# The sub-norm weights of differential attention, applied in the copies out of the turned blocks

## The chip, the cores and the metric

One core of one Trainium2 chip runs the whole program. The metric is device time in microseconds (us) of one execution; the number quoted for a kernel is the median of several runs.

## The reference, cut to what matters

The program runs six layers over 256 tokens of width 1024, all in fp32: two hybrid layers (the second with a mixture of eight experts), then a layer of differential attention, one of block attention, one of sliding-window attention, and differential attention again. The change touches the two differential layers (numbers 2 and 5 of the kernel). What they compute after the attention itself is this:

```python
def rms_norm(x, g):
    xf = x.astype(jnp.float32)
    y = xf * lax.rsqrt(jnp.mean(xf * xf, axis=-1, keepdims=True) + NORM_EPS)
    return (y * g.astype(jnp.float32)).astype(x.dtype)

def diff_attention(...):
    ...
        p = p[:, :, 0] - lam * p[:, :, 1]
        return jnp.einsum('bhqk,bkhe->bqhe', p.astype(v.dtype), v)
    ...
    o = rms_norm(o, sub_g) * (1.0 - lambda_init)
    return o.reshape(B, S, H * DIFF_V_DIM) @ w_out
```

There are 8 heads of 128 columns. The weights `sub_g` are 128 numbers, the same for all heads, one for each column of a head.

## The kernel before, in words

**Products.** Every product with a weight matrix is made of three fp32r products. A unit of weights (128x2048) is loaded by the queue of SP into one of six buffers `raw`; ScalarE rounds it into `whi` (`hi`, line 1691, or half a unit at a time at line 1695), VectorE takes the remainder into `wlo` (`lo`, lines 2116 and 2122), and TensorE adds high by high, low by high and high by low. The activations are split in the same way: rows of `y` are turned by TensorE into a bank of PSUM, ScalarE copies the bank, rounded, into `xt_hi`, VectorE subtracts that from the bank into `xt_lo`. For the output product of attention these three steps are the three functions named `turn_mixed` (lines 798, 1711 and 2140), called for s = 0 to 3. In a differential layer s = 0 and 1 turn heads 0 to 3 of the first and of the second half of the tokens, s = 2 turns heads 4 and 5 and s = 3 heads 6 and 7, for all tokens. After turning, a partition of `xt` holds one column of a head.

**Attention in a differential layer** (`soft_heads`, 16 score maps in 8 pairs) is software-pipelined by hand: each engine has its own written-out order of steps. TensorE computes scores (lines 1593 and 1595), VectorE masks them and takes maxima (line 2551), ScalarE takes exponentials with row sums (lines 1821 and 1823), VectorE takes reciprocals (line 2500), GpSimd makes the ratio of the two maps (`ratio`, lines 711 and 712), VectorE combines the pair in two instructions (`combine`, line 2471), TensorE turns the combined map (`turn_pair`, line 1568), ScalarE copies it (line 1839), TensorE multiplies by the values (`pair_values`, lines 1580 to 1582), and VectorE scales the result into `y` (`finish_pair`, line 2482), sums its squares (line 2486) and asks GpSimd for a root (line 2150). In between TensorE does the last parts of the projection of the layer (line 843).

**The sub-norm** is `diff_norms` on GpSimd. For each head it makes the ratio of a later head, the root (line 692), then two passes over the head's 128x256 block of `y`: a multiplication by the root of each row (line 729) and one by the weights (line 730). The second raises `normed`, on which TensorE's `turn_mixed` waits (after 4, 4, 6 and 8 heads). The weights come in `subg`, 2 x 128 numbers copied to all partitions by one transfer (line 594, in `small`), and are scaled once by 1 - lambda_init (line 2425).

**Output product.** `out_project_diff` (line 977) orders the work of TensorE after the last pair: rows of the first half of the tokens for units 0 and 1, `turn_mixed` for s = 2, a part for the second half, `turn_mixed` for s = 3, then unit 2 once the low part of s = 2 is there and unit 3 once that of s = 3 is there. ScalarE and VectorE come to the two halves of unit 3 (`hi` and `lo` with halves) only after their own part of `turn_mixed` for s = 3.

```python
            for h in range(8):
                if h + 2 < 8:
                    ratio(l, h + 2)
                r = done[0]
                roots(1)
                pool.wait_ge(root_ready, r + 1)
```

Of the kernel before, what the change touches and what calls it, by code (L numbers as in the profile page):

```python
# [6 lines left out]
F32 = mybir.dt.float32  # L7
# [7 lines left out]
P = 128  # L15
# [157 lines left out]
def build(nc, A, out, bias_scratch):  # L173
    with ExitStack() as ctx:  # L174
        def sb(name, shape, dt=F32, scope=ctx):
            return scope.enter_context(nc.sbuf_tensor(name, shape, dt))
# [15 lines left out]
        sinks = sb("sinks", [P, 16])  # L192
        minus_sinks = sb("minus_sinks", [P, 16])
        lam = sb("lam", [P, 16])
        subg = sb("subg", [P, 2, 2 * HD])
        pos_i = sb("pos_i", [P, NT], I32)
        rope_f = sb("rope_f", [P, 6, NT, 8])
        rope_k = sb("rope_k", [P, NT, 8], I32)
# [216 lines left out]
        def mixed_bank(l, s):  # L415

            b = bank[turned_at(l)[s]]
            return (b[:, :].rearrange("p (k s) -> p k s", k=4) if s < 2 and KIND[l] != HYB else
                    b[:, :].rearrange("p (t k s) -> p t k s", t=NT, k=2))

        def mixed_cols(x_t, l, s):
            if s < 2 and KIND[l] != HYB:
                return x_t[:, 0:4, s * P:(s + 1) * P]
            n = mixed_block(l, s)
            return x_t[:, 2 * n:2 * n + 2, :].rearrange("p k (t s) -> p t k s", t=NT)
# [112 lines left out]
        def _(sp):  # L538
# [50 lines left out]
            def small():  # L589
                sp.dma_start(pos_i[:], A["positions_2"][0].rearrange("(t p) -> p t", p=P),  # L590
                             allow_slow_non_contiguous=True).then_inc(got["pos"], 16)
                for i, n in enumerate(("diff_lam_q1_2", "diff_lam_k1_2", "diff_lam_q2_2", "diff_lam_k2_2")):
                    sp.dma_start(lam_in[:, i], A[n].partition_broadcast(P)).then_inc(got["lam"], 16)
                sp.dma_start(subg[:], A["diff_subln_g_2"].partition_broadcast(P)).then_inc(got["subg"], 16)
                sp.dma_start(router_w[:], A["moe_router"][0].rearrange("(k p) e -> p k e", p=P)).then_inc(
                    got["router"], 16)
                sp.dma_start(sinks[:], A["swa_sinks_2"][0].partition_broadcast(P)).then_inc(got["sinks"], 16)
# [84 lines left out]
        @block.gpsimd  # L682
        def _(pool):
            pool.wait_ge(cst_loaded, 16)
            done = [0]

            def roots(n):
                for _ in range(n):
                    r = done[0]
                    w = ROOTS[r]  # L690
                    pool.wait_ge(var_ready, r + 1)
                    pool.tensor_tensor(rstd[:, r % 8, 0:w], var[:, r % 8, 0:w], cst[:, C_HALF:C_HALF + w],  # L692
                                       ALU.pow).then_inc(root_ready, 1)
                    done[0] += 1

            def stick_masks(l):
                for p in range(NSTICK[KIND[l]] // 2):
                    pool.wait_ge(z_read, HEAD0[l] + 2 * p + 2)
                    if p < 2:

                        pool.wait_ge(qk_turned, HEAD0[l] // 2 + 3)
                    else:
                        pool.wait_ge(pool_out, l + 1)
                    pool.tensor_tensor(stick_a(p), stick_z(p), stick_mask(C_STRICTNEG), ALU.add).then_inc(zm_ready, 1)

            def ratio(l, h):

                d = DIFF_SLOT[l]
                pool.wait_ge(var_ready, done[0] + 1)
                second = rinv[:, :, 2 * h + 1:2 * h + 2]  # L710
                link(pool.tensor_tensor(second, second, sums[:, :, 2 * h:2 * h + 1], ALU.mult))
                pool.tensor_tensor(second, second, lam[:, 10 + d:11 + d].rearrange("p c -> p c ()").broadcast_to([P, NT, 1]),
                                   ALU.mult).then_inc(root_ready, 1)
                done[0] += 1

            def diff_norms(l):

                ratio(l, 0)
                ratio(l, 1)
# [5 lines that stand above are left out]
                    pool.wait_ge(root_ready, r + 1)  # L725
                    v = y[:, :, h * P:(h + 1) * P]
                    scale = rstd[:, r % 8, 0:NT].rearrange("p t -> p t ()").broadcast_to([P, NT, P])
                    gains = subg[:, DIFF_SLOT[l]].rearrange("p c -> p () c").broadcast_to([P, NT, P])
                    link(pool.tensor_tensor(v, v, scale, ALU.mult))
                    ins = pool.tensor_tensor(v, v, gains, ALU.mult)  # L730
                    ins.then_inc(normed, 1)

            chain = [0]

            def link(ins):

                chain[0] += 1
                ins.then_inc(pchain, 1)
                pool.wait_ge(pchain, chain[0])

            for l in range(NL):
                if KIND[l] != HYB:
                    roots(2)
                if KIND[l] == SWA:
                    pool.wait_ge(rope_sin, 1)
                    pool.wait_ge(proj_ev, EV0[l + 1])
                    rotate(pool, link, [(8, 8)], late_tmp).then_inc(late_rope_done, 1)
                stick_masks(l)
                if KIND[l] == DIFF:
                    diff_norms(l)  # L750
                if l == 1:
                    roots(2)
                    pool.wait_ge(t_lo, 4 * 5)
                    for t in range(NT):
                        for half in range(2):
                            pool.memset(y[:, t, half * 512:(half + 1) * 512], 0.0).then_inc(added, 1)
                    roots(4)
                else:
                    roots(6 if KIND[l] == HYB else 2)
            roots(2)  # L760
# [913 lines left out]
        def _(act):  # L1674
# [33 lines left out]

            def turn_mixed(l, s):
                act.wait_ge(turned, 4 * (3 * l + 1) + s + 1)  # L1710
                act.activation(mixed_cols(xt_hi, l, s), mixed_bank(l, s), ACT.Copy).then_inc(t_hi, 1)

            def high_of_tokens(t):
                act.activation(xn_hi[:, t], x[:, t], ACT.Copy).then_inc(xn_hi_ready, 1)
# [384 lines left out]
        def _(dve):  # L2099
# [4 lines left out]
            def link(ins):  # L2104

                chain[0] += 1
                ins.then_inc(dchain, 1)
                dve.wait_ge(dchain, chain[0])
# [28 lines left out]

            def turn_mixed(l, s):
                dve.wait_ge(t_hi, 4 * (3 * l + 1) + s + 1)
                dve.tensor_tensor(mixed_cols(xt_lo, l, s), mixed_bank(l, s), mixed_cols(xt_hi, l, s).bitcast(F32),  # L2140
                                  ALU.subtract).then_inc(t_lo, 1)

            def ask_root(src, scale, eps, w):

# [245 lines left out]
            def setup():  # L2390
# [31 lines left out]
                    link(dve.tensor_scalar(lam[:, 10 + d:11 + d], lam[:, 8 + d:9 + d], -LAMBDA_INIT[l], None, ALU.add))  # L2422
                dve.wait_ge(got["subg"], 16)
                for l, d in DIFF_SLOT.items():
                    link(dve.tensor_scalar(subg[:, d], subg[:, d], 1.0 - LAMBDA_INIT[l], None, ALU.mult))

            def add_bias(l, c, t):

# [575 lines left out]
```

## Time and profile before

| | us |
|---|---|
| median of 3 runs | 2429.32 (2429.15 to 2430.7) |
| the profiled execution, its own time | 2427.38 |
| span of its trace, first to last instruction | 2425.6 |
| TensorE busy | 2393.6 (99% of the span) |
| VectorE busy | 1725.7 (71%) |
| ScalarE busy | 1450.1 (60%) |
| GpSimd busy | 94.3 (4%) |
| mean granted TensorE clock | 0.999 |

An engine is busy while one of its instructions runs; waiting, branching and issuing transfers are not counted. Matmuls are pipelined, each is drawn with the latency of its end, so two of them that follow without a gap overlap in the trace (a 128x512 fp32r product is drawn with 0.39 us, and the next one starts 0.23 us after it). A gap between two of them is therefore larger for the engine than the idle time that the trace shows. PE is TensorE, PEld its loading of weights, DVE is VectorE, ACT ScalarE, POOL GpSimd. `L730` is line 730 of the kernel. A row of the timeline gives the start in us from the start of the span, the duration of the merged group in us, engine, line, operation, tiles with shapes and count, and in brackets how long the engine was idle ahead of it and what ended that.

### The profile page before, as it was taken

How to read it: one execution, taken by the hardware profiler on the slowest of the kernel's cores; microseconds unless marked ns; L12 is line 12 of the kernel's file. 1: busy time of each engine (PE TensorE's matmuls, PEld its weight loads, DVE VectorE, ACT ScalarE, POOL GpSimd, SP SyncE). 2: the span in 40 equal slices, each digit the busy share in tenths (PEclk: the TensorE clock that was granted, in tenths of full speed). 3: DMA queues.
4: the chain of work that ended last, by engine and by line, in shares of the span. 5: the costliest groups of instructions: out<-in, count | busy, mean ns of one | idle time of the engine just before them, and what ended most of it. 6: DMA issues, size and time to landing. Idle time of an engine off the chain costs nothing. (4 is left out here: it accounts for less than half of the span.)

```text
span 2425.6 us, 31990 instructions
## 1 busy us (share of the span) xinstructions
PE 2393.6 (99%) x12546; PEld 2017.5 (83%) x12546; DVE 1725.7 (71%) x1911; ACT 1450.1 (60%) x1662; POOL 94.3 (4%) x130
## 2 busy tenths in 40 slices
PE   9999999999999999999999999999999999999998
PEld 7889978888888888888877788888888788887887
DVE  5565456888898998988995865666656665568565
ACT  6454354588888888888865554454444554456442
POOL 1000010000000000000000300000000000004000
PEclk9999999999999999999999999999999999999999
DMA  9266552699999999999965365452655265553553
GB/s 323 69 204 206 181 208 72 223 348 361 348 350 359 335 360 352 348 350 347 363 244 193 105 217 191 156 200 95 223 191 187 72 211 191 172 205 119 186 191 104
DMA packets 242366, 555.40 MB, mean 229 GB/s; under 512 B 10841, under 2 KB 36849, under 8 KB 241905
## 3 DMA queue, kind: packets, MB, share of 16 engines
q1 hardware_dynamic: 242160, 552.41, 65.5%
q8 instruction: 159, 2.61, 0.4%
q14 instruction: 47, 0.38, 0.0%
HBM read 551.31 MB, written 1.07 MB: 228 GB/s over the span
## 5 line engine op out<-in xcount | busy, mean ns | idle before, releaser
L2116 DVE TENSOR_TENSOR wlo<-raw,whi 128x2048 fp32r<-128x2048 f32 x486 | 1112.8, 2297 | 444.8 <-ACT whi L1691 444.0
L1691 ACT ACTIVATE whi<-raw 128x2048 fp32r<-128x2048 f32 x487 | 933.7, 1925 | 551.2 <-PE bank L921 141.6
L843 PE MATMUL bank<-whi,xt 128*128 128x512 f32 (+1 forms) x1056 | 311.3, 379 | 3.3 <-DVE xt L2133 1.3
L843 PEld LDWEIGHTS bank<-whi,xt 128*128 128x128 f32 x1056 | 189.5, 188 | 40.6 <-issue 3.1
L1234 PE MATMUL bank<-whi,xt 128*128 128x512 f32 (+1 forms) x768 | 222.0, 373 | 0.8 <-DVE e_hf L2744 0.8
L1077 PE MATMUL bank<-xt,whi 128*128 128x512 f32 x768 | 209.1, 394 | 0.0
L843 PE MATMUL bank<-wlo,xt 128*128 128x512 f32 (+1 forms) x528 | 197.6, 374 | 0.0
L921 PE MATMUL bank<-whi,h_hi 128*128 128x512 f32 x596 | 184.8, 391 | 0.0
L921 PE MATMUL bank<-whi,h_lo 128*128 128x512 f32 x596 | 183.9, 390 | 0.0
L921 PE MATMUL bank<-wlo,h_hi 128*128 128x512 f32 x596 | 183.9, 390 | 0.0
L1234 PEld LDWEIGHTS bank<-whi,xt 128*128 128x128 f32 x768 | 138.2, 189 | 24.8 <-DVE e_hf L2744 1.2
L1077 PEld LDWEIGHTS bank<-xt,whi 128*128 128x128 f32 x768 | 133.0, 189 | 19.1
L1234 PE MATMUL bank<-whi,odd_hi 128*128 128x512 f32 (+1 forms) x384 | 144.0, 375 | 0.1
L1234 PE MATMUL bank<-wlo,odd_hi 128*128 128x512 f32 (+1 forms) x384 | 142.9, 372 | 0.0
L1234 PE MATMUL bank<-wlo,xt 128*128 128x512 f32 (+1 forms) x384 | 142.8, 372 | 0.0
L1234 PE MATMUL bank<-whi,odd_lo 128*128 128x512 f32 (+1 forms) x384 | 142.7, 372 | 0.0
L921 PEld LDWEIGHTS bank<-whi,h_lo 128*128 128x128 f32 x596 | 111.9, 188 | 23.9
L921 PEld LDWEIGHTS bank<-wlo,h_hi 128*128 128x128 f32 x596 | 111.9, 188 | 23.7
L1081 PEld LDWEIGHTS bank<-xt,wlo 128*128 128x128 f32 x768 | 117.8, 189 | 16.2
L921 PEld LDWEIGHTS bank<-whi,h_hi 128*128 128x128 f32 x596 | 109.3, 188 | 20.6
L1081 PE MATMUL bank<-xt,wlo 128*128 128x256 f32 x768 | 122.1, 281 | 0.0
L692 POOL TENSOR_TENSOR rstd<-var,cst 128x1 f32<-128x1 f32 (+2 forms) x46 | 37.2, 808 | 2065.8 <-DVE var L2150 2051.1
(345 smaller groups left out, 3834.4 us busy)
## 6 DMA issues: line engine op xcount, KB each, us to landing
raw<-in_moe_wg SPq DMA_DIRECT2D x88, 1024.0 KB, 6.1
raw<-in_moe_wu SPq DMA_DIRECT2D x88, 1024.0 KB, 5.8
raw<-in_moe_wd SPq DMA_DIRECT2D x88, 1024.0 KB, 5.9
raw<-in_mlp_w_up SPq DMA_DIRECT2D x64, 1024.0 KB, 5.3
raw<-in_mlp_w_down SPq DMA_DIRECT2D x64, 1024.0 KB, 4.9
raw<-in_diff_w_in SPq DMA_DIRECT2D x24, 1024.0 KB, 5.2
raw<-in_w_in SPq DMA_DIRECT2D x19, 1024.0 KB, 7.8
raw<-in_moba_w_in SPq DMA_DIRECT2D x12, 1024.0 KB, 5.1
```

Source lines behind the costliest of these rows:

```text
L692: pool.tensor_tensor(rstd[:, r % 8, 0:w], var[:, r % 8, 0:w], cst[:, C_HALF:C_HALF + w], ALU.pow).then_inc(root_ready, 1)
L843: mm = pe.matmul(proj_bank(l, c, t)[:, 0:width], a[:, kx, t * P:(t + 1) * P], b[:, k, :], start=(kx == 0 and i == 0), stop=(kx == KT - 1 a ...
L921: mm = pe.matmul(bank[4 + 2 * t + half][:, :], a[:, k, t * P:(t + 1) * P], b[:, kk, half * 512:(half + 1) * 512], start=begin and i == 0, ...
L1077: pe.matmul(bank[f][:, :], hi[:, k, f * P:(f + 1) * P], xt[:, :, kx, :], start=kx == 0, stop=False, skip_group_check=True)
L1081: mm = pe.matmul(bank[f][:, 0:S], lo[:, k, f * P:(f + 1) * P], xt_hi[:, kx, :], start=False, stop=kx == KT - 1, skip_group_check=True)
L1234: mm = pe.matmul(bank[b][:, 0:width], a[:, kx, t * P:(t + 1) * P], w[:, k, :], start=(kx == 0 and i == 0), stop=(kx == KT - 1 and i == 2))
L1691: act.activation(whi[u % NH][:, :], raw[u % NR][:, :], ACT.Copy).then_inc(hi_ready[u % NR], 2)
L2116: dve.tensor_tensor(wlo[u % NR][:, :], raw[u % NR][:, :], whi[u % NH][:, :].bitcast(F32), ALU.subtract).then_inc(lo_ready[u % NR], 2)
```

## The change

The weights are no longer copied to all partitions: `subg` holds one factor per partition, in one column for each of the two layers, and is loaded so (element by element). GpSimd makes only the multiplication by the root and signals `normed` from it. In the copies of `turn_mixed`, for differential layers, ScalarE multiplies by the factor of the partition (an activation named Identity with a per-partition scale in place of Copy), and VectorE computes bank times factor minus high part in one `scalar_tensor_tensor`. For s = 2 and 3 that is two instructions, one for each half of the tokens. The factor 1 - lambda_init is applied to the columns as before. The tile `subg` shrinks from 256 to 32 numbers per partition, so that the tiles allocated after it lie 896 bytes lower.

```diff
--- before.py
+++ after.py
@@ -192,7 +192,7 @@
         sinks = sb("sinks", [P, 16])
         minus_sinks = sb("minus_sinks", [P, 16])
         lam = sb("lam", [P, 16])
-        subg = sb("subg", [P, 2, 2 * HD])
+        subg = sb("subg", [P, 32])
         pos_i = sb("pos_i", [P, NT], I32)
         rope_f = sb("rope_f", [P, 6, NT, 8])
         rope_k = sb("rope_k", [P, NT, 8], I32)
@@ -591,7 +591,8 @@
                              allow_slow_non_contiguous=True).then_inc(got["pos"], 16)
                 for i, n in enumerate(("diff_lam_q1_2", "diff_lam_k1_2", "diff_lam_q2_2", "diff_lam_k2_2")):
                     sp.dma_start(lam_in[:, i], A[n].partition_broadcast(P)).then_inc(got["lam"], 16)
-                sp.dma_start(subg[:], A["diff_subln_g_2"].partition_broadcast(P)).then_inc(got["subg"], 16)
+                sp.dma_start(subg[:, 0:2], A["diff_subln_g_2"].rearrange("d p -> p d"),
+                             allow_slow_non_contiguous=True).then_inc(got["subg"], 16)
                 sp.dma_start(router_w[:], A["moe_router"][0].rearrange("(k p) e -> p k e", p=P)).then_inc(
                     got["router"], 16)
                 sp.dma_start(sinks[:], A["swa_sinks_2"][0].partition_broadcast(P)).then_inc(got["sinks"], 16)
@@ -725,10 +726,7 @@
                     pool.wait_ge(root_ready, r + 1)
                     v = y[:, :, h * P:(h + 1) * P]
                     scale = rstd[:, r % 8, 0:NT].rearrange("p t -> p t ()").broadcast_to([P, NT, P])
-                    gains = subg[:, DIFF_SLOT[l]].rearrange("p c -> p () c").broadcast_to([P, NT, P])
-                    link(pool.tensor_tensor(v, v, scale, ALU.mult))
-                    ins = pool.tensor_tensor(v, v, gains, ALU.mult)
-                    ins.then_inc(normed, 1)
+                    pool.tensor_tensor(v, v, scale, ALU.mult).then_inc(normed, 1)
 
             chain = [0]
 
@@ -1708,7 +1706,9 @@
 
             def turn_mixed(l, s):
                 act.wait_ge(turned, 4 * (3 * l + 1) + s + 1)
-                act.activation(mixed_cols(xt_hi, l, s), mixed_bank(l, s), ACT.Copy).then_inc(t_hi, 1)
+                gain = subg[:, DIFF_SLOT[l]:DIFF_SLOT[l] + 1] if KIND[l] == DIFF else 1.0
+                act.activation(mixed_cols(xt_hi, l, s), mixed_bank(l, s), ACT.Identity if KIND[l] == DIFF else ACT.Copy,
+                               scale=gain).then_inc(t_hi, 1)
 
             def high_of_tokens(t):
                 act.activation(xn_hi[:, t], x[:, t], ACT.Copy).then_inc(xn_hi_ready, 1)
@@ -2137,8 +2137,18 @@
 
             def turn_mixed(l, s):
                 dve.wait_ge(t_hi, 4 * (3 * l + 1) + s + 1)
-                dve.tensor_tensor(mixed_cols(xt_lo, l, s), mixed_bank(l, s), mixed_cols(xt_hi, l, s).bitcast(F32),
-                                  ALU.subtract).then_inc(t_lo, 1)
+                if KIND[l] == DIFF:
+                    gain = subg[:, DIFF_SLOT[l]:DIFF_SLOT[l] + 1]
+                    parts = [(mixed_cols(xt_lo, l, s), mixed_bank(l, s), mixed_cols(xt_hi, l, s))]
+                    if s > 1:
+                        parts = [tuple(a[:, t] for a in parts[0]) for t in range(NT)]
+                    for low, src, high in parts:
+                        ins = dve.scalar_tensor_tensor(out=low, in0=src, scalar=gain, in1=high.bitcast(F32),
+                                                       op0=ALU.mult, op1=ALU.subtract)
+                    ins.then_inc(t_lo, 1)
+                else:
+                    dve.tensor_tensor(mixed_cols(xt_lo, l, s), mixed_bank(l, s),
+                                      mixed_cols(xt_hi, l, s).bitcast(F32), ALU.subtract).then_inc(t_lo, 1)
 
             def ask_root(src, scale, eps, w):
 
@@ -2422,7 +2432,7 @@
                     link(dve.tensor_scalar(lam[:, 10 + d:11 + d], lam[:, 8 + d:9 + d], -LAMBDA_INIT[l], None, ALU.add))
                 dve.wait_ge(got["subg"], 16)
                 for l, d in DIFF_SLOT.items():
-                    link(dve.tensor_scalar(subg[:, d], subg[:, d], 1.0 - LAMBDA_INIT[l], None, ALU.mult))
+                    link(dve.tensor_scalar(subg[:, d:d + 1], subg[:, d:d + 1], 1.0 - LAMBDA_INIT[l], None, ALU.mult))
 
             def add_bias(l, c, t):
```

## Rows read from the trace of the kernel before

**Rows 1.** Page, part 1: busy us, share of the span, instructions.

```profile
PE 2393.6 (99%) x12546; PEld 2017.5 (83%) x12546; DVE 1725.7 (71%) x1911; ACT 1450.1 (60%) x1662; POOL 94.3 (4%) x130
```

**Rows 2.** Busy time by stretch, us and counts, PE, PEld, DVE, ACT, POOL, clock, DMA.

```profile
1330.00:1370.00 40.00, 37.32 (x224) 29.52 (x223) 32.80 (x117) 24.25 (x69) 22.43 (x36) 1.00 0.17 54
2190.00:2230.00 40.00, 37.37 (x220) 29.76 (x218) 32.23 (x114) 23.24 (x67) 22.40 (x36) 1.00 0.16 54
```

**Rows 3.** TensorE's waits, 2190 to 2230: us in total, times, longest.

```profile
PE bank L1568 <- DVE z L2471: 1.5, 2, 1.2
PE bank L798 <- POOL y L730: 0.4, 1, 0.4
```

**Rows 4.** Line 730, whole span: duration in ns min/median/max, first and last start.

```profile
L730 POOL TENSOR_TENSOR y<-y,subg x16: 722/732/889, 1335.1 to 2222.1; 128x256 f32<-128x256 f32 x16
```

**Rows 5.** Timeline of VectorE in layer 5, the pairs of `combine`.

```profile
2188.55 0.74 DVE L2471 SCALAR_TENSOR_TENSOR z<-z,rinv 128x128 f32<-128x128 f32 x2
...
2193.41 1.74 DVE L2471 SCALAR_TENSOR_TENSOR z<-z,rinv 128x128 f32<-128x128 f32 x2
...
2203.80 1.72 DVE L2471 SCALAR_TENSOR_TENSOR z<-z,rinv 128x128 f32<-128x128 f32 x2
...
2207.69 1.10 DVE L2471 SCALAR_TENSOR_TENSOR z<-z,rinv 128x128 f32<-128x128 f32 x2
```

**Rows 6.** Timeline of GpSimd beside the second of these pairs.

```profile
2193.44 0.61 POOL L729 TENSOR_TENSOR y<-y,rstd 128x256 f32<-128x256 f32 x1
2194.14 0.73 POOL L730 TENSOR_TENSOR y<-y,subg 128x256 f32<-128x256 f32 x1
```

**Rows 7.** Timeline of TensorE, scores (L1595) and turned map (L1568), twice.

```profile
2194.31 0.60 PE L1595 MATMUL bank<-qk 64*128 64x256 f32 x4
2195.20 0.55 PE L1568 MATMUL bank<-cst,z 128*128 128x128 f32 x3 [0.28 <-DVE z L2471]
...
2199.84 0.60 PE L1595 MATMUL bank<-qk 64*128 64x256 f32 x4
2200.37 0.55 PE L1568 MATMUL bank<-cst,z 128*128 128x128 f32 x3
```

**Rows 8.** Timeline of TensorE from the seventh pair to unit 3 of the output.

```profile
2212.18 0.55 PE L1568 MATMUL bank<-cst,z 128*128 128x128 f32 x3 [1.22 <-DVE z L2471]
...
2221.89 0.63 PE L921 MATMUL bank<-wlo,xt 128*128 128x512 f32 x2
...
2222.89 0.66 PE L798 MATMUL bank<-cst,y 128*128 128x128 f32 x4 [0.37 <-POOL y L730]
...
2226.53 1.16 PE L921 MATMUL bank<-whi,xt 128*128 128x512 f32 x4 [0.22 <-DVE wlo L2122]
```

**Rows 9.** Groups by line and shape, whole span: busy us, mean ns, idle before.

```profile
L1711 ACT ACTIVATE xt<-bank 128x512 fp32r<-128x512 f32 x24 | 13.9, 595 | 40.8 <-PE bank L798 40.6
...
L1765 ACT ACTIVATE y<-y,cst 128x768 f32<-128x768 f32 x4 | 3.7, 931 | 0.0
L1762 ACT ACTIVATE y<-y 128x768 f32<-128x768 f32 x4 | 3.4, 848 | 0.1
...
L2773 DVE SCALAR_TENSOR_TENSOR y<-bank,gw,y 128x512 f32<-128x512 f32 x28 | 19.9, 746 | 0.2
...
L2140 DVE TENSOR_TENSOR xt<-bank,xt 128x512 fp32r<-128x512 f32 x24 | 16.2, 688 | 20.5 <-ACT xt L1711 20.3
...
L2482 DVE TENSOR_TENSOR y<-bank,rinv 128x256 f32<-128x256 f32 x16 | 6.6, 415 | 1.0 <-PE bank L1582 1.0
```

**Rows 10.** The same view of ScalarE: one of the loads of an activation table.

```profile
L1862 ACT ACT_TABLE_LOAD x1 | 1.3, 1283 | 0.0
```

**Rows 11.** Timeline of the queue of SP, after the small transfers of layer 0.

```profile
70.13 1.47 SPq L597 DMA_DIRECT2D sinks<-in_swa_sinks  x1
78.58 12.57 SPq L555 DMA_DIRECT2D raw<-in_ffn_wg  x2
```

## Prediction

> **What bounds the kernel now.** I read the page first: TensorE is busy 2393.6 of 2425.6 us [rows 1], so whatever the change does to the other engines counts only where TensorE waits for them. It touches two layers only, so the second view is the busy time of the two stretches in which their attention ends [rows 2]. They are alike to 0.1 us: 40 us long, 37.3 to 37.4 of TensorE, 32 to 33 of VectorE, 22.4 of GpSimd, with the transfers at 17%. The granted clock is 1.00, the level of 2.4 GHz, and nothing here puts it in question. TensorE stands idle 2.68 and 2.63 us, 5.3 us in both; this is about all that a change in this place could give. The third view says for whom it waits [rows 3]: mostly for VectorE's combined pairs (1.5 us, one wait of 1.2), and 0.4 us for line 730, the pass that the change removes. Everything below is worked out for layer 5 and holds for layer 2 too, whose timeline repeats it.
>
> **What is removed.** Sixteen passes of 0.73 us on GpSimd [rows 4], 11.7 us in all. GpSimd has idle time, so the sum isn't a gain; two things are. The first is the direct one: a head's block is ready 0.73 us sooner, plus a step of 0.08 between the passes. The second is a side effect that I found by comparing the same instructions of VectorE. The two that combine a pair take 0.74 us beside an idle GpSimd, 1.10 beside one of its passes, and 1.74 or 1.72 where both passes lie beside them [rows 5]; the pair that starts at 2193.41 ends at 2195.15, just after line 730's pass has run from 2194.14 to 2194.87 [rows 6]. So the second pass costs VectorE some 0.62 us where it falls on such a pair, which it does three times in a layer.
>
> **The path, step by step.** Only what TensorE then starts sooner counts.
> - Second long pair: the turning of the map (L1568) normally starts 0.53 us after the scores (L1595), 2200.37 against 2199.84; here it starts 0.89 after them [rows 7]. With a pair of 1.10 us VectorE ends at 2194.51, ahead of 2194.31 + 0.53 = 2194.84. Gain 0.36.
> - Seventh pair: VectorE runs almost without a gap from the long pair at 2203.80 to the pair that TensorE awaits at 2212.18, for 1.22 us [rows 5, 8]. If the first comes 0.62 earlier, so does the last. The passes by the roots (L729) stay and still lie beside it, so the wait doesn't go away: it gets shorter by 0.62. Right behind it TensorE needs the low part of s = 0, which is now the longer instruction (below), 0.06 more. Gain 0.56.
> - s = 3: the last two products start at 2221.89 and 2222.12, so that the turned block could start at 2222.35; it starts at 2222.89, released by line 730 [rows 8]. Its block comes over 0.8 us sooner now. Gain 0.54.
> - Unit 3: its first product (2226.53) had waited for its low half [rows 8], which ScalarE and VectorE make after their own parts of s = 3. The distance of 3.64 us from the turned block therefore stays, and grows by what the copies grow: loss 0.08 for ScalarE's, and 0.05 that I allow for the low part of s = 2, which comes close to its deadline once the wait ahead of it is gone. Loss 0.13.
> - Sum 0.36 + 0.56 + 0.54 - 0.13 = 1.33 us in a layer, 2.7 in both. Behind it TensorE is the bound again and carries the gain to the end.
>
> **What is added.** ScalarE's copy of 595 ns gets a per-partition scale. The nearest rows are two activations on 768 columns, 931 ns with one operand read per partition and 848 without [rows 9]: 83 ns. Bounds: nothing, and 0.17 if the bias of Identity is such an operand too; a gain is excluded, since it reads more. I take 0.08, as Relu and Copy with their fixed bias show no more. The Trainium skill ("ScalarE: Activation LUTs", What ACT_TABLE_LOAD costs) says that each such operand adds about 93 ns to an activation, near the 83 of the row; with two operands by its figure the loss at unit 3 would be 0.19 and the sum 2.4 us in place of 2.7. VectorE's instruction: 746 ns for bank, factor and tensor against 688 for the present one [rows 9], so 0.06 more for s = 0 and 1. For s = 2 and 3 it is two on 256 columns each; 415 ns for a plain one [rows 9] plus 58 makes 0.95 us at most, one undivided 0.75 at least, against 0.69. I take 0.9, or 0.2 more. At s = 3 it is covered: ScalarE rounds the first half of unit 3 meanwhile, which has twice the columns of the block. Without that cover it would cost the same 0.2 a layer. Queued behind these copies are, on ScalarE, the exponentials of the last two maps at s = 0, whose sums VectorE reads over 1 us later, and on VectorE the scaling of the sixth pair's result.
>
> **Edits that I cost at nothing.** The element-wise load of the factors sits in the queue of SP ahead of the router's weights and the sinks; SP then waits until 78.58 for a free buffer, 7 us after the last of them [rows 11]. A load slower by less than that is hidden; its result is read over 100 us later. The scaling by 1 - lambda_init gets shorter, in layer 0, off the path. The shift of the tiles by 896 bytes has no row of its own. The nearest is line 730 on eight blocks of `y`: least and median duration are 722 and 732 ns [rows 4], so place made 10 ns at most, either way; I take none.
>
> **The rivals.**
> - *Only the direct wait goes* (chance 0.14). VectorE's chain has slots that wait for row sums of ScalarE or for scores, and if these come last there, 0.62 less at one pair ends in another wait. For it: VectorE's share is under 82% of the stretch. Then 0.54 - 0.13 = 0.4 a layer, 0.8 us in all: 2428.5.
> - *No effect at all* (0.06). TensorE does other products meanwhile, and the longer copies eat up the rest: 2429.3. Against it is the 0.54 at s = 3, whose releaser is the very instruction that goes.
> - *All the waits open* (0.12). VectorE and GpSimd shift so far that the passes of line 729 no longer fall on the pairs. Then the 5.3 us of rows 2 go, and a little at each seam: 2424.0. Against it: the root and its pass follow the same request as before, so they keep their place beside the next pair.
> - *Slower: Identity needs another activation table than the exponential* (0.06). The place is s = 0, between exponentials: a load of 1.283 us [rows 10] ahead of the copy, one back, one more for s = 1, and one back in the next attention. That is four for layer 2 and three for layer 5, which has no attention behind it: 9.0 us. With all on the path and the gain kept it comes to 9.0 - 2.7 = 6.3 us more, 2435.6. It turns slower than 0.2% only from six of the seven on the path, (2.7 + 4.9) / 1.283. Against it: VectorE and TensorE have other work at s = 1. The Trainium skill ("ScalarE: Activation LUTs", Table sets) states that cheap functions, identity among them, are in every set as filler; by that rule no load is added, and no run here shows it yet.
>
> **The numbers.** The forecast (chance 0.62) is 2.7 us less. Against the profiled execution's own 2427.38 us (span 2425.6) that is 2424.7. The median shown, 2429.32, lies 1.94 above that execution, and on this scale the forecast is 2426.7; its own bounds are 2425.2 (another long pair counts, no loss at the copies) and 2428.0 (0.17 for ScalarE, 0.2 uncovered for VectorE, half the gain at the seventh pair). About 0.2%, 4.9 us, is what a measurement of this kernel can tell from no change. The range of 2423.8 to 2430.0 takes in the forecast, the first three rivals and the spread of the runs; it leaves out the table loads and what I haven't thought of. Faster by over 0.2% is the third rival and a little: 0.13. Slower by over 0.2%: 0.06. The same: 0.81.
>
> **What would show it.** In the trace after: line 729 at 0.61 us with no pass behind it; no pair at L2471 of 1.7 us; no wait of L798 for GpSimd; the wait of L1568 at 0.6 in place of 1.2; L1711's activations at about 0.68 us, L2140's successor at 0.75 and twice 0.47; the two stretches of rows 2 with 1.3 us less idle TensorE each. Wrong would be: more table loads on ScalarE, the long pairs still there (then GpSimd's second pass wasn't their cause), or a new wait of L921 for the low part of s = 2 or 3 of more than 0.3 us.

## The result, and the profile after

The forecast of 2426.7 us (2423.8 to 2430.0) was wrong, and on the wrong side. The changed kernel takes 2445.63 us, the median of 4 runs (2445.36 to 2448.47), against 2429.24 us for the kernel before: a ratio of 1.0071 [1.0059, 1.0084], so 16.4 us slower. The span of the profiled execution is 2443.6 us, 18.0 more than before, at a mean granted clock of 1.0 (0.999 before).

The page, part 1, after. It answers to [rows 1].

```profile
PE 2412.4 (99%) x12546; PEld 2018.9 (83%) x12546; DVE 1722.1 (70%) x1915; ACT 1450.6 (59%) x1662; POOL 82.3 (3%) x114
```

The count of TensorE's instructions is the same to the last one, 12546, and they take 18.8 us more (2412.4 against 2393.6). GpSimd lost what it should lose, 12.0 us in 16 instructions. So the time isn't in a wait: TensorE does the same work more slowly. The view that shows where is the one of groups by line and shape. (The lines of TensorE's code are two lower after the change: L921 is L919, L1234 is L1232, L1312 is L1310, L843 is L841.) The columns are busy us, mean ns of one, and idle time before. Before:

```profile
L843 PE MATMUL bank<-whi,xt 128*128 128x512 f32 x896 | 281.4, 395 | 2.5 <-DVE xt L2133 1.3 <-DVE wlo L2116 1.0 <-DVE wlo L2918 0.2
...
L921 PE MATMUL bank<-whi,h_hi 128*128 128x512 f32 x596 | 184.8, 391 | 0.0
...
L1234 PE MATMUL bank<-whi,odd_lo 128*128 128x512 f32 x320 | 124.6, 389 | 0.0
...
L1312 PE MATMUL bank<-whi,e_lo 128*128 128x512 f32 x352 | 109.2, 389 | 0.0
```

After:

```profile
L841 PE MATMUL bank<-whi,xt 128*128 128x512 f32 x896 | 281.3, 395 | 2.6 <-DVE wlo L2116 1.1 <-DVE xt L2133 1.1 <-DVE wlo L2928 0.4
...
L919 PE MATMUL bank<-whi,h_hi 128*128 128x512 f32 x596 | 187.8, 396 | 0.0
...
L1232 PE MATMUL bank<-whi,odd_lo 128*128 128x512 f32 x320 | 126.3, 395 | 0.0
...
L1310 PE MATMUL bank<-whi,e_lo 128*128 128x512 f32 x352 | 111.2, 395 | 0.0
```

The name ahead of the comma is the moving operand, the one behind it the stationary one. Products of a weight buffer (moving, 512 columns) with `xt` (stationary) are unchanged within 1 ns, group by group: 395 ns for the group shown, 390 to 398 for the others. Those with `h_hi`, `h_lo`, `odd_hi`, `odd_lo`, `e_hi` and `e_lo` as stationary operand went from 389 to 393 ns up to 394 to 398, each by 4 to 6, and are called 390 and 395 below: nine groups, 3 x (596 + 320 + 352) = 3804 products, whose busy times sum to 19.6 us more, 5.2 ns for each. They belong to the feed-forward and expert parts, where the change touches no line. What it did touch is where these tiles lie. `subg` shrank from 1024 to 128 bytes of a partition, and every tile declared behind it lies 896 bytes lower; `whi`, `wlo`, `xt`, `x` and `y` are declared ahead of it and stay.

At the place that the prediction was about, the change did what was forecast. Groups of GpSimd, ScalarE and VectorE after:

```profile
L729 POOL TENSOR_TENSOR y<-y,rstd 128x256 f32<-128x256 f32 x16 | 10.0, 624 | 1.3
L1710 ACT ACTIVATE xt<-bank,subg 128x512 fp32r<-128x512 f32 x8 | 5.5, 688 | 14.0 <-PE bank L796 14.0
L2146 DVE SCALAR_TENSOR_TENSOR xt<-bank,subg,xt 128x256 fp32r<-128x256 f32 x8 | 3.5, 480 | 5.1 <-ACT xt L1710 5.1
L2146 DVE SCALAR_TENSOR_TENSOR xt<-bank,subg,xt 128x512 fp32r<-128x512 f32 x4 | 3.0, 745 | 0.0
```

TensorE's waits for the pairs, whole span, after. Before they came to 3.0 us in four waits. The two for line 730, 0.7 us before, are gone.

```profile
PE bank L1566 <- DVE z L2481: 2.3, 2, 1.2
```

### The profile page after: what moved, and what is told of

Read it like the earlier page. It is cut to its first block and busy times, and to the rows that moved or that the text cites. A ratio compares the mean times of both kernels' runs of the same rounds, so it can differ in the third digit from the quotient of the medians.

```text
span 2443.6 us, 31978 instructions
## 1 busy us (share of the span) xinstructions
PE 2412.4 (99%) x12546; PEld 2018.9 (83%) x12546; DVE 1722.1 (70%) x1915; ACT 1450.6 (59%) x1662; POOL 82.3 (3%) x114
## 5 line engine op out<-in xcount | busy, mean ns | idle before, releaser
L841 PE MATMUL bank<-whi,xt 128*128 128x512 f32 (+1 forms) x1056 | 311.3, 379 | 3.4 <-DVE wlo L2116 1.1
L1232 PE MATMUL bank<-whi,xt 128*128 128x512 f32 (+1 forms) x768 | 222.1, 374 | 0.9 <-DVE e_hf L2754 0.8
L841 PEld LDWEIGHTS bank<-whi,xt 128*128 128x128 f32 x1056 | 189.6, 188 | 40.2 <-issue 2.7
L841 PE MATMUL bank<-wlo,xt 128*128 128x512 f32 (+1 forms) x528 | 197.5, 374 | 0.0
L919 PE MATMUL bank<-whi,h_hi 128*128 128x512 f32 x596 | 187.8, 396 | 0.0
L919 PE MATMUL bank<-whi,h_lo 128*128 128x512 f32 x596 | 187.0, 395 | 0.0
L919 PE MATMUL bank<-wlo,h_hi 128*128 128x512 f32 x596 | 186.9, 394 | 0.0
L1232 PEld LDWEIGHTS bank<-whi,xt 128*128 128x128 f32 x768 | 138.2, 188 | 25.1 <-DVE e_hf L2754 1.2
L1075 PEld LDWEIGHTS bank<-xt,whi 128*128 128x128 f32 x768 | 133.0, 189 | 19.6
L1232 PE MATMUL bank<-whi,odd_hi 128*128 128x512 f32 (+1 forms) x384 | 145.5, 379 | 0.1
L1232 PE MATMUL bank<-wlo,odd_hi 128*128 128x512 f32 (+1 forms) x384 | 144.3, 376 | 0.0
L1232 PE MATMUL bank<-whi,odd_lo 128*128 128x512 f32 (+1 forms) x384 | 144.3, 376 | 0.0
L1232 PE MATMUL bank<-wlo,xt 128*128 128x512 f32 (+1 forms) x384 | 143.0, 372 | 0.0
L919 PEld LDWEIGHTS bank<-whi,h_lo 128*128 128x128 f32 x596 | 112.2, 188 | 26.5
L919 PEld LDWEIGHTS bank<-wlo,h_hi 128*128 128x128 f32 x596 | 112.1, 188 | 26.5
L1079 PEld LDWEIGHTS bank<-xt,wlo 128*128 128x128 f32 x768 | 117.8, 189 | 16.2
L919 PEld LDWEIGHTS bank<-whi,h_hi 128*128 128x128 f32 x596 | 109.6, 188 | 23.1
L1079 PE MATMUL bank<-xt,wlo 128*128 128x256 f32 x768 | 122.2, 281 | 0.0
L841 PEld LDWEIGHTS bank<-wlo,xt 128*128 128x128 f32 x528 | 99.4, 188 | 18.1
```

The source lines that it names most:

```text
L841: mm = pe.matmul(proj_bank(l, c, t)[:, 0:width], a[:, kx, t * P:(t + 1) * P], b[:, k, :], start=(kx == 0 and i == 0), stop=(kx == KT - 1 a ...
L919: mm = pe.matmul(bank[4 + 2 * t + half][:, :], a[:, k, t * P:(t + 1) * P], b[:, kk, half * 512:(half + 1) * 512], start=begin and i == 0, ...
L1075: pe.matmul(bank[f][:, :], hi[:, k, f * P:(f + 1) * P], xt[:, :, kx, :], start=kx == 0, stop=False, skip_group_check=True)
L1079: mm = pe.matmul(bank[f][:, 0:S], lo[:, k, f * P:(f + 1) * P], xt_hi[:, kx, :], start=False, stop=kx == KT - 1, skip_group_check=True)
L1232: mm = pe.matmul(bank[b][:, 0:width], a[:, kx, t * P:(t + 1) * P], w[:, k, :], start=(kx == 0 and i == 0), stop=(kx == KT - 1 and i == 2))
```

## The experiments

Three questions: is it the place of the tiles alone; which places are bad; and what is the change worth once the place is taken out of it? The padding experiments on the kernel of before add a line or two that allocate an unused tile, and change no instruction. Addresses are bytes within a partition, worked out from the sizes of the tiles in the order of their declaration, each begun at a multiple of 32 bytes; no trace shows them, and only their differences matter below. Those of the weight buffers are 128 more than a multiple of 256 (`whi` begins at 65664) and so are, before, those of `xt` (98432), `h_hi` (167040) and `odd_hi` (209024). The kernel before was measured again beside each set of experiments: 2428.46 us beside the first four below, 2428.65 beside 256 bytes, the one pair, `xt` and the removal alone, and 2428.67 beside the others.

### The changed kernel with the tile of the factors as large as before

```diff
-        subg = sb("subg", [P, 32])
+        subg = sb("subg", [P, 256])
```

> The changed kernel, but the tile subg keeps its 256 numbers per partition (two are used), so that every tile lies where it lay before the change. Theory A, the place of the tiles: in the changed kernel the 128x512 products whose stationary operand is h_hi, h_lo, e_hi, e_lo, odd_hi or odd_lo take 395 ns in place of 390, 19 us in all; here they are back at 390, and the time is 2445.6 - 19.2 = 2426.4 us, below the kernel before. Theory B, the code: the longer copies on ScalarE and VectorE or another order of the instructions slow TensorE down; then the time stays near 2445 us and the products at 395 ns.

Measured: 2427.11 us (11 runs), ratio 0.9994 [0.9984, 1.0003]; the nine groups are back at 390 to 393 ns, as before. All of the loss is the layout. The median lies 1.4 us under the kernel before where 2.7 were forecast, and its interval would allow for no gain too; this is taken up below.

### The kernel of before, moved by 128 and by 512 bytes

```diff
         subg = sb("subg", [P, 2, 2 * HD])
+        pad = sb("pad", [P, 32])
```

> The kernel before, with an unused tile of 128 bytes behind subg, so that the tiles after it lie 128 bytes higher. The change moved them by -896 bytes, which is the same modulo 1024. Theory A with the place counting modulo 1024: products with a moved stationary operand at 395 ns, 2429.2 + 19.2 = 2448 us. Theory A with another period, or with the direction of the move counting: something between 2429 and 2448 us. Theory B: 2429 us, nothing changes.

Measured: 2447.95 us, ratio 1.0081 [1.0066, 1.0097]. One unused tile of 128 bytes in an otherwise unchanged kernel costs 19.5 us. The nine groups show 394 to 396 ns (`odd_hi` with `whi` 398, 393 before), everything else is as before. With `[P, 128]` in place of `[P, 32]`, 512 bytes:

> The kernel before with an unused tile of 512 bytes behind subg. If only the distance from the moving operand whi or wlo modulo 512 or less counts: 2429 us, products at 390 ns, as in the kernel before. If the distance modulo 1024 or more counts: the products with a moved stationary operand differ from 390 ns, and the time from 2429 us by 3.8 us for each ns. Theory B: 2429 us.

Measured: 2428.62 us, ratio 0.9998 [0.9989, 1.0008]; products at 390. That a tile lies elsewhere is harmless; some places are bad.

### Everything moved together by 128 bytes

```diff
+        pad = sb("pad", [P, 32])
         with ExitStack() as loads:
             raw = [sb(f"raw{s}", [P, 2048], scope=loads) for s in range(NR)]
```

> The kernel before with an unused tile of 128 bytes ahead of raw, so that all large tiles, moving and stationary, lie 128 bytes higher and keep their distances. If the distance between the stationary and the moving operand is what counts: 2429 us, all products at 390 ns. If the place of the stationary operand by itself counts: at least 2448 us, and the products from xt (lines 843, 1234 with xt, 1098) are at 395 ns too, some 2600 more of them, 13 us: about 2461 us. Theory B: 2429 us.

Measured: 2426.76 us, ratio 0.9995 [0.9986, 1.0004], and 390 ns. `h_hi` now has the same place within 256 bytes as in the changed kernel (a multiple of 256), and is fast; what differs is that the weight buffers moved with it. What counts isn't where the stationary operand lies but how far it is from the moving one.

### Distances of 256, 64 and 32 bytes more

The line of the second experiment, with `[P, 64]`, `[P, 16]` and `[P, 8]`.

> The kernel of before with 256 bytes of padding behind the factors, so that the tiles behind them lie 256 bytes further from whi and xt. 128 bytes cost 19 us, 512 bytes nothing. Theory A (only a distance that is a whole number of the 512 bytes of one stationary operand is fast): h, odd and e products at 395 ns, about 2447 us. Theory B (the period is 256 bytes or less): products at 390 ns, 2428.5 us. I give A 0.5.

> The kernel of before with 64 bytes of padding behind the factors. 128 bytes cost 19 us, 256 and 512 nothing. Theory A (every distance off the multiples of 256 bytes costs the same): products with h, odd and e at 395 ns, 2447.5 us. Theory B (the cost grows with the distance from the nearest multiple): 392 to 393 ns, 2438. Theory C (the multiples of 64 that aren't one of 128 are no worse than 0): 2428.5. I give A 0.4, B 0.3, C 0.3.

> The kernel of before with 32 bytes of padding behind the factors. Theory A (every distance off the multiples of 256 bytes costs the same): 395 ns, 2447.5 us. Theory B (in proportion): 391 ns, 2433. Theory C (small shifts don't count): 390 ns, 2428.5.

| tiles behind `subg` moved by | us | ratio | product with `h_lo`, ns |
|---|---|---|---|
| +32 bytes | 2449.96 | 1.0093 [1.0078, 1.0109] | 395 |
| +64 | 2449.77 | 1.0088 [1.0072, 1.0103] | 395 |
| +128 | 2447.95 | 1.0081 [1.0066, 1.0097] | 395 |
| +256 | 2429.07 | 0.9999 [0.9989, 1.0008] | 390 |
| +512 | 2428.62 | 0.9998 [0.9989, 1.0008] | 390 |
| -896 (the change) | 2445.63 | 1.0071 [1.0059, 1.0084] | 395 |

I had given "only whole multiples of 512" a chance of 0.5, and it fell: 256 is as good as nothing. And the price isn't in proportion to the distance: 32 and 64 bytes cost no less than 128. Their medians are 2 us higher; the three intervals overlap, but the busy times of the nine groups grew in the same order, by 22.8, 21.5 and 19.5 us. So theory A of the last two expectations holds, theories B and C fell, and the 2 us stay unexplained. In the distances tried the rule is a difference that is a multiple of 256 bytes or not; 896 is three times 256 and 128 more.

### Only one pair of tiles moved

```diff
+            pad = sb("pad", [P, 32], scope=moe_scope)
             odd_hi = sb("odd_hi", [P, KT, S], F32R, scope=moe_scope)
```

> The kernel of before with 128 bytes of padding ahead of odd_hi alone, so that only odd_hi and odd_lo move. If the loss belongs to the tile that moved: the three groups of 320 products with odd_hi or odd_lo go from 390 to 395 ns (3 x 320 x 5 ns = 4.8 us), those with h_hi, h_lo, e_hi and e_lo stay at 390; about 2433 us. Rival (the loss is one of the whole layout, such as where everything ends): all groups move, 2448, or none does, 2428.5.

Measured: 2433.35 us, ratio 1.0019 [1.0010, 1.0029], against 2433 expected. In the groups by shape only the products with the moved tiles slow down, by 5.2 us of busy time in all:

```profile
L922 PE MATMUL bank<-wlo,h_hi 128*128 128x512 f32 x596 | 183.8, 390 | 0.0
...
L1235 PE MATMUL bank<-whi,odd_lo 128*128 128x512 f32 x320 | 126.2, 394 | 0.0
...
L1313 PE MATMUL bank<-whi,e_lo 128*128 128x512 f32 x352 | 109.2, 390 | 0.0
```

So the loss adds up product by product and isn't a matter of where the whole layout ends.

### `xt` moved by 128 bytes, the other tiles by 512

```diff
+        pad = sb("pad", [P, 32])
         xt = sb("xt", [P, 2, KT, S], F32R)
...
         subg = sb("subg", [P, 2, 2 * HD])
+        pad2 = sb("pad2", [P, 96])
```

> The kernel of before with 128 bytes of padding ahead of xt and 384 more behind the factors: xt lies 128 bytes further from whi and wlo, the tiles behind the factors 512 further, which was harmless. If the distance between the stationary and the moving operand is what counts: the products of L843, L1234, L1098 and L921 that have xt as stationary operand (of 512 columns: 896 + 448 + 640 + 320 + 320 + 160 + 376 + 188 = 3348) go from 390 to 395 ns, about 16.7 us more; those with h, odd and e stay at 390; those of L1077 with xt stationary and whi moving (768 of 512 columns) may go with them, 3.8 us more. So 2445 to 2449 us. Rival (only the tiles behind the factors can be hurt): 2428.5.

Measured: 2441.23 us, ratio 1.0053 [1.0038, 1.0069]. The pattern is turned round: what was slow in the changed kernel is fast, and what was untouched there is slow.

```profile
L845 PE MATMUL bank<-whi,xt 128*128 128x512 f32 x896 | 285.3, 399 | 2.5 <-DVE xt L2135 1.3 <-DVE wlo L2118 0.8 <-DVE wlo L2920 0.4
...
L1079 PE MATMUL bank<-xt,whi 128*128 128x512 f32 x768 | 210.3, 395 | 0.0
L1236 PE MATMUL bank<-whi,xt 128*128 128x512 f32 x640 | 201.9, 397 | 0.7 <-DVE e_hf L2746 0.5 <-issue 0.2
...
L923 PE MATMUL bank<-wlo,h_hi 128*128 128x512 f32 x596 | 183.9, 390 | 0.0
```

The size was off: 12.6 us against 16.7 and more, and the time is outside the 2445 to 2449 us expected. The busy times of the groups with `xt` stationary grew by 14.7 us in all, 4.4 ns a product and not 5; and the span grew by 13.1 us where TensorE's busy time grew by 15.1 (2408.7 against 2393.6), so that 2 us were covered by time in which TensorE had waited (its waits, as listed, sum to 22.8 us in place of 24.9). The group in which `xt` is the moving operand and `whi` the stationary one (L1079, L1077 before) grew by 1.2 us for 768 products, 1.6 ns each and less than the others. The slower place of `xt` at 98560 is the one it had, without loss, when everything was moved together: the same address, another distance.

### The removal alone, and the copies alone

The kernel of before, its layout kept, without the pass over the rows; the weights are left out of the result.

```diff
-                    gains = subg[:, DIFF_SLOT[l]].rearrange("p c -> p () c").broadcast_to([P, NT, P])
-                    link(pool.tensor_tensor(v, v, scale, ALU.mult))
-                    ins = pool.tensor_tensor(v, v, gains, ALU.mult)
-                    ins.then_inc(normed, 1)
+                    pool.tensor_tensor(v, v, scale, ALU.mult).then_inc(normed, 1)
```

> The kernel of before without GpSimd's pass over the rows with the sub-norm's weights; nothing takes its place, so the weights are left out of the result. Layout and copies as before. It prices the removal alone. If the prediction's working holds (pairs of 1.7 us gone, the wait for GpSimd at s = 3 gone, no added cost at the copies): 1.46 us a layer less, 2.9 in both, about 2425.8 us. Rival, from the run with the full tile: the earlier start is given back where TensorE's granted clock falls behind the wait at the seventh pair, so 1 to 1.5 us less in all, 2427.2.

Measured: 2426.34 us (11 runs), ratio 0.9988 [0.9979, 0.9997]. That is 2.3 us less, with an interval of about 1 to 5 us. The expectation said 2.9 and, for its rival, 1 to 1.5; the interval takes in both, so this run doesn't decide between them.

The changed kernel with the full tile and a second pass on GpSimd, which multiplies by the roots once more and so gives another result (the line of the first experiment, and this):

```diff
-                    pool.tensor_tensor(v, v, scale, ALU.mult).then_inc(normed, 1)
+                    link(pool.tensor_tensor(v, v, scale, ALU.mult))
+                    pool.tensor_tensor(v, v, scale, ALU.mult).then_inc(normed, 1)
```

> The changed kernel with the full tile for the factors (distances as before) and with a second pass of GpSimd put back behind the first: it multiplies by the reciprocal roots once more in place of the weights, so the result is another, the instructions on GpSimd are those of before. It prices the new copies alone. By the prediction's working 0.13 us a layer, 0.26 in all: 2428.8 us. Rival: the copies (688 against 594 ns on ScalarE, 745 and twice 440 on VectorE against 688) sit on TensorE's path more than was taken, and eat the difference between the run with the full tile and the one without the pass, 0.8 us or more: 2429.3 or above.

Measured: 2428.06 us (11 runs), ratio 0.9998 [0.9989, 1.0007]. The expected 0.1 us of loss can't be told from none, but the rival, 0.6 us or more of loss beside this chip's 2428.67, isn't supported. It is not a clean price of the copies either: GpSimd is busy 92.6 us here, not the 94.3 of before, since the pass that was put back is the shorter one.

### The change, with the distance mended

```diff
         subg = sb("subg", [P, 32])
+        pad = sb("pad", [P, 32])
```

> The changed kernel as it is, with 128 bytes of padding behind the small tile of factors: the tiles behind lie 768 bytes lower than before, a whole number of 256 bytes. If a distance that is a multiple of 256 bytes is what the products need, all of them are back at 390 ns and the time is that of the run with the full tile, 2427.1 us (2426 to 2428), against 2445.6 for the change as it was made. If not, near 2445.

Measured: 2426.26 us (11 runs, 2424.78 to 2427.26), ratio 0.9991 [0.9982, 1.0000], within the 2426 to 2428 us expected and 19.4 us under the change as it was made. The tiles lie 768 bytes lower than before, three times 256. The interval against the kernel before just reaches 1, so by the times alone the gain of 2.4 us is at the edge of what these runs can tell; the distances in the traces, below, show it more sharply.

## Why the prediction was wrong

**The step that failed** is the last of the edits costed at nothing: "The shift of the tiles by 896 bytes has no row of its own ... place made 10 ns at most, either way; I take none." That the 5 ns which place made here lie inside that bound is luck: the bound is one of GpSimd's pass, not of a product, and it left out that row's longest duration, 889 ns. What failed is that I took it from one pass of GpSimd and left it there, without the count of the instructions that the shift reaches. With it failed the sentence that the prediction opens with, that a change counts only where TensorE waits: this one made TensorE's own instructions longer. The shift reaches 3804 products of the engine that bounds the kernel, which has no idle time to hide them. 5 ns x 3804 is 19 us, seven times the 2.7 us forecast for everything else. Even the bound as I had it, 10 ns by 3804, would have been 38 us and the widest term of the sum. The nearest row was also the wrong one: the eight blocks compared there differ by multiples of 512 bytes, which the runs show to be harmless for TensorE's products, and no row that I had read before the result has a product at another distance.

**The rivals.** None of them held. The one on the slower side was about loads of activation tables; no load was added. The sign of the result was right only there, for another reason.

**The mechanism in attention**, step by step, can be judged in the mended kernel, whose only difference from the change is the padding. Two rows of TensorE's timeline in layer 5 set the base, 2184.48 before and 2185.20 in the mended kernel. Before:

```profile
2184.48 0.55 PE L1568 MATMUL bank<-cst,z 128*128 128x128 f32 x3
```

The mended kernel (L1567 turns the map, L797 the rows of `y`, L920 are the output products; columns as in [rows 7]):

```profile
2185.20 0.55 PE L1567 MATMUL bank<-cst,z 128*128 128x128 f32 x3
...
2195.56 0.55 PE L1567 MATMUL bank<-cst,z 128*128 128x128 f32 x3
...
2212.14 0.55 PE L1567 MATMUL bank<-cst,z 128*128 128x128 f32 x3 [1.15 <-DVE z L2482]
...
2221.92 0.63 PE L920 MATMUL bank<-wlo,xt 128*128 128x512 f32 x2
2222.39 0.60 PE L797 MATMUL bank<-cst,y 128*128 128x128 f32 x4
...
2226.07 1.17 PE L920 MATMUL bank<-whi,xt 128*128 128x512 f32 x4 [0.17 <-DVE wlo L2123]
```

| distance from the base, us | before [rows 7, 8] | mended | step | forecast |
|---|---|---|---|---|
| second long pair | 10.72 | 10.36 | -0.36 | -0.36 |
| seventh pair | 27.70 | 26.94 | -0.40 | -0.62 |
| turned block, s = 3 | 38.41 | 37.19 | -0.46 | -0.48 |
| unit 3 | 42.05 | 40.87 | +0.04 | +0.13 |
| sum | | | -1.18 | -1.33 |

The 0.06 us for the low part of s = 0 fall behind the start of the seventh pair (its products follow after 0.66 us in place of 0.60), so that the forecast of -0.56 is written here as -0.62 and +0.06. In layer 2 the whole distance goes from 42.12 to 40.93 us, 1.19 less, and in the changed kernel as it was made it is 40.90 in layer 2 and 40.87 in layer 5: the gain is there too, under the loss. Both layers make 2.4 us, which is also what the median of the mended kernel shows (2428.67 - 2426.26). So the working of these steps stands in the main, with three sizes off, by 0.22, 0.02 and 0.09 us.

- *The pairs.* VectorE's pairs were to take 1.10 us in place of 1.74 [rows 5]. In layer 5 of the mended kernel (start us, us, engine, line):

```profile
2189.27 0.74 DVE L2482 SCALAR_TENSOR_TENSOR z<-z,rinv 128x128 f32<-128x128 f32 x2
...
2194.13 1.19 DVE L2482 SCALAR_TENSOR_TENSOR z<-z,rinv 128x128 f32<-128x128 f32 x2
...
2204.33 1.18 DVE L2482 SCALAR_TENSOR_TENSOR z<-z,rinv 128x128 f32<-128x128 f32 x2
...
2207.72 1.10 DVE L2482 SCALAR_TENSOR_TENSOR z<-z,rinv 128x128 f32<-128x128 f32 x2
```

No pair is left at 1.7. The same instruction costs 0.74, 1.10 to 1.19, or 1.72 to 1.74 us beside none, one or two passes of GpSimd. The Trainium skill ("GPSIMD Engine Reference", Specifications) says that GpSimd shares its SBUF interfaces with VectorE, in contention with instructions that have two SBUF inputs; this one has them, and the traces agree. The three former long pairs now take 1.18 or 1.19, not 1.10. The last of them also starts only 0.19 us sooner (19.13 us behind the base, 19.32 before), not the 0.36 by which TensorE had come forward. These 0.08 and 0.17 are the 0.22 missing at the seventh pair, to within 0.03.

- *The wait at the seventh pair* was to be 0.6 us in place of 1.2, and it is 1.15. The gain is there all the same, since TensorE itself arrives 0.69 us sooner (25.79 us behind the base, 26.48 before): 0.36 from the second long pair, the rest from small waits on the way that opened too, such as 0.20 us for `nmx` ahead of the scores of the last pair. I had taken the gain of VectorE as one of this wait alone. The start moves by the right amount, the length of the wait doesn't.
- *s = 3.* Line 797 starts right behind the two products that start at 2221.92, at 2222.39 and with no wait. As forecast.
- *The copies.* ScalarE's takes 688 ns (0.68 forecast), VectorE's 745 and twice 480 (0.75 and twice 0.47 forecast). The sum at unit 3 is 0.04 rather than 0.13. The Trainium skill ("ScalarE: Activation LUTs", What ACT_TABLE_LOAD costs) says 93 ns for an operand read per partition; 688 - 595 is 93 here, and it is one such operand, not two. The rule that the prediction cites from the Trainium skill ("ScalarE: Activation LUTs", Table sets), that identity is in every set, holds here also: no load was added, there are 12 in either trace.
- *The load of the factors* element by element was hidden, as forecast: no group of waits of the changed kernel names it, and in the mended kernel it landed 5.6 us after its issue, against 6.3 for the larger one before.
- *Idle time in the two stretches* was to fall by 1.3 us each. As drawn it fell by 0.7 (TensorE busy 38.05 and 38.12 us of 40 in the mended kernel, 37.32 and 37.37 before, with the stretches moved along with the base), while the distances shrank by 1.2. A gap is drawn shorter than the engine feels it, so idle time was the wrong sign to name.

**The clock behind the seventh pair.** By their medians the full tile gave 1.4 us, the removal alone 2.3 and the mended kernel 2.4. The intervals overlap widely, so no difference between the three is shown. But in the profiled execution of each of the first two, one of the two layers lost 1.6 us again. TensorE's timeline in layer 5 with the full tile, behind the wait at the seventh pair; before, the same four products took 1.20 us:

```profile
2211.02 0.55 PE L1566 MATMUL bank<-cst,z 128*128 128x128 f32 x3 [1.15 <-DVE z L2481]
2211.68 1.93 PE L919 MATMUL bank<-whi,xt 128*128 128x512 f32 x4
```

and the windows of that run (PE busy, granted clock, DMA share, GB/s):

```profile
2205.00:2210.00 5.00, 4.42 (x34) 1.00 0.55 191
2210.00:2215.00 5.00, 3.87 (x13) 0.69 0.01 2
2215.00:2220.00 5.00, 5.00 (x31) 0.97 0.02 3
```

Behind a wait of 1.15 us the mean granted clock of 5 us is 0.69, so that a part of them ran at the lower of the two levels, 1.2 GHz, and the way from the seventh pair to the turned block of s = 1 takes 4.40 us (2211.02 to 2215.42) in place of 2.75. In the run without the pass it is layer 2, where the same way takes 4.34 us:

```profile
1355.00:1360.00 5.00, 5.00 (x25) 0.73 0.00 0
```

The mended kernel has the same instructions as the one with the full tile and shows 1.00 in both layers, with waits of 1.18 and 1.15 us, and so does the changed kernel. So neither the length of the wait nor the code alone decides it. Over all traces, the clock fell in two of the eight stretches of the four kernels without the second pass, and in none of the twenty of the ten kernels that have two passes (the kernel before, its padded forms and the copies alone, with waits of 1.14 to 1.22 us). Whether the removal makes the fall more likely or this is chance stays open; 1.6 us is more than one layer's gain, so it would matter. By the profile with the full tile alone, one would look for the missing gain in the copies or the pairs, where it isn't.

**The numbers.** The range had no room for 16 us because no rival had a mechanism that acts outside the two stretches of [rows 2]; every one of them was placed beside the edited lines. Without the shift the forecast of 2.7 us less would have come close (2.4 measured).

## What to carry to other kernels

An edit that changes the size of a tile moves every tile declared behind it, and so edits instructions that aren't in the diff. Where it can reach the engine that bounds the kernel, multiply the unknown by the count of those instructions before calling it nothing, or keep the layout with padding. In a kernel of fp32r products of 512 columns, try to keep stationary and moving operand a multiple of 256 bytes apart within a partition; it costs a line of padding, and here it is worth 19 us in 2426. Products of 256 columns don't ask for it, and other types were not tried. When a result is off, look first at whether the bounding engine did the same count of instructions at another mean, which the groups by line and shape show, and which points to the operand.

## What the runs showed of the hardware that was not expected

- A product of 128x128 by 128x512 (fp32r) takes 390 ns where the distance between the stationary and the moving operand is a multiple of 256 bytes (0, 256, 512, -768 bytes from the layout before) and 395 ns where it isn't (32, 64, 128, -896). The absolute place doesn't matter: both moved by 128 bytes, 390. By busy time the price is 5.1 ns at 128 bytes and 6.0 at 32. Why it is so, no run here shows. Nor do they tell whether the moving operand's distance to the product's own stationary operand counts, or to the next one, which is loaded beside it (in the trace before, that of the product which starts at 2190.96 was loaded from 2190.73 on, while the two products begun at 2190.41 ran until 2191.12): in these groups both lie in the same tiles or in tiles moved together.
- Products of 256 columns don't show it, they are rather drawn a little shorter. In the changed kernel `odd_lo` with 256 columns takes 281 ns, against 283 before (278 with 64 bytes of padding), while with 512 columns it goes from 389 to 395. The 32 products of `xt` with `perm_t`, of 512 columns and with `perm_t` moved by 896 bytes, have a median of 395 ns against 394 before: they didn't take part, and why is open. The group with `xt` as the moving operand at the wrong distance paid 1.6 ns.
- The loading of the stationary operand isn't longer: 188 ns for `h_hi` before and after. Only the products are.
